# Attention output sums of a two-layer model: full-precision matmuls for the differential heads, one matmul per block with stationary values for the stick-breaking heads

## Chip, cores and metric

The kernel runs on one core of one Trainium2 chip. The metric is the device time of one execution in microseconds (us), the median of several runs; before the change it is 3962.36 us over three runs.

## What is computed

Two layers over 2048 tokens of width 1024. The first has three token mixers side by side (a pooling mixer, differential attention, stick-breaking attention) and a gated feed-forward network; the second has a gated spatial mixer and retention. The change touches the sums of values in the two attentions of the first layer:

```python
# differential attention, 4 heads; two softmaxes of width 64, values of width 128
attn = p[:, :, 0] - lam * p[:, :, 1]
outs.append(jnp.einsum('bhqk,bkhe->bqhe', attn, vb))
# stick-breaking attention, 4 heads of width 64, strictly causal
suffix = lax.cumsum(log_1mb, axis=3, reverse=True) - log_1mb
a = jnp.where(mask, jnp.exp(jax.nn.log_sigmoid(z) + suffix), 0.0)
outs.append(jnp.einsum('bhqk,bkhd->bqhd', a, vb))
```

Both are causal: a tile of 128 queries reads only the keys up to its own end.

## The kernel before

All data is float32. TensorE has a reduced format, fp32r, and the kernel keeps precision by splitting a number x into hi (x rounded to fp32r) and lo (x - hi, in fp32r) and adding up products: three matmuls for a projection (`product`, L1325 to L1327), fewer where one side needs less.

**Order of the work.** `order_of_work` runs once, in Python, and writes out a list of steps; each engine's program takes the steps of its own kinds in that order and waits for the others by semaphores. Two generators are interleaved: `projections` (all dense products, norms and gates) and `attention`. Their yields carry planned costs (`softmax_cost`, `sticks_cost`), by which attention steps are spread between the dense ones. `in_halves(n, fn)` puts a step n half-steps later. None of the costs is changed.

**Attention** goes through the 2048 tokens in four chunks c of 512 (CT). Heads j = 0 to 3 are the differential ones; j = 4 and 5 are pairs of stick-breaking heads, r = 0 and 1 in a pair. For each head and each tile qt of 128 queries it walks over blocks kb of keys of width w (512, or 128 to 512 on the diagonal). For a block:

- `scores` (L1424, L1425): TensorE, into PSUM bank 4 or 5;
- the weights: for differential heads a maximum on VectorE, Exp on ScalarE (L1649), a scaling on GpSimd and the difference of the two maps on VectorE (L1961); for stick-breaking heads logs, a scan and an Exp;
- `turn_p` (L1433): TensorE turns the weights in pieces of 128 columns, by transposes into PSUM bank 6. There is one such bank (`tring`, one place), so the next `turn_p` waits until bank 6 has been read;
- `split_p`: ScalarE copies bank 6 as hi (L1662), VectorE then writes lo = bank 6 - hi (L1967), both into tile PT, which has two places (`pt`);
- `pv` (L1447, L1449), two half-steps after `turn_p`: the turned weights are stationary, the values stream past them. For each 128 keys hi is loaded and streams [values hi, values lo], then lo is loaded and streams values hi. A differential head has 128 value columns, so 256 and 128 columns stream; a stick-breaking head has 64, so 128 and 64 stream. All add up in PSUM bank 7 (`oring`, one place);
- `take_out` (L1976), at the end of a tile: VectorE adds the halves of bank 7 into OB. The next tile's first `pv` waits for it.

There are 16 query tiles per head and 136 pieces of 128 by 128 (16 * 17 / 2), so 544 pieces for the four differential heads and 544 for the four stick-breaking ones. By blocks that is 160 each: 112 of four pieces, and 16 each of one, two and three.

When a head is done, `finish_head` squares it on ScalarE (L1690), norms and stores it.

**Values.** The value projection leaves a 128 by 512 bank; ScalarE writes hi to a staging tile, VectorE lo (`store_v`, L1884), and ScalarE's queue stores both to the DRAM scratch VS (`put_v`). `load_v` on the sync engine's queue (SP) loads 512 KB per block into the KV buffer.

The change's names in the order tables below: BIG, WF and W are operands of the dense products, KV and QQ keys, values and queries, PP the weights before they are turned, PT and PTW the turned ones, CB constants (the identity matrix among them), OB the head outputs, PS PSUM.

## Time and profile before

| | |
|---|---|
| three runs | 3962.36, 3954.04, 3963.06 us (median 3962.36) |
| span of the profiled execution | 3954.2 us |
| TensorE busy | 3727.1 us (94%), mean granted clock 0.978 |
| TensorE weight loads | 3270.0 us (83%) |
| VectorE, ScalarE, GpSimd busy | 1989.4, 1700.0, 799.3 us |
| HBM | 591.49 MB read, 179.59 MB written |

The profile comes from one execution. Its page gives the span, from the first to the last record, and no separate total for that execution; the median of the runs stands 8.2 us above the span. "PE" is TensorE's matmuls, "PEld" its weight loads, which overlap the matmuls. The duration of a matmul record contains its way through the pipeline, so matmuls that follow each other overlap in the records: what a matmul costs is read from the distance between starts. Line numbers (L1447) are those of the kernel before.

### The profile page before, as it was taken

The page shows a single profiled execution, that of the slowest core. Times are in us where ns is not written, and L with a number is a line of the kernel's source. Part 1 is how long each engine was busy: PE and PEld are TensorE (multiplying, and loading weights), DVE is VectorE, ACT ScalarE, POOL GpSimd, SP SyncE. Part 2 cuts the span into 40 slices and gives each one's busy share as a digit, 9 for nine tenths or more (in the row PEclk, how much of TensorE's full clock was granted, in tenths as well). Part 3 has the DMA queues.
Part 4 walks back from the last instruction along what each step waited for, and adds up shares of the span by engine and source line. Part 5 has one row for each costly group of instructions (what it writes and reads, how often), then busy time and mean ns, then how long its engine had stood idle before and what let it go on. Part 6 is the DMA issues. An engine that isn't in the chain of part 4 may idle for free.

```text
span 3954.2 us, 56218 instructions
## 1 busy us (share of the span) xinstructions
PE 3727.1 (94%) x21768; PEld 3270.0 (83%) x21768; DVE 1989.4 (50%) x4259; ACT 1700.0 (43%) x3455; POOL 799.3 (20%) x704
## 2 busy tenths in 40 slices
PE   7999899999998999999999999999999989999998
PEld 6888788787878887888888987888879987888897
DVE  4446575556646565555646545444566743101343
ACT  4334455556644444445544434334555543111322
POOL 3443333454444331100001000111000000000100
PEclk9999999999999999999999999999999999999999
DMA  6886667676666567454444555555353445555453
GB/s 171 276 270 184 191 206 276 223 266 233 241 238 210 208 208 277 173 174 165 164 171 159 176 192 208 181 181 179 132 201 124 142 157 212 192 192 191 163 187 143
DMA packets 327706, 774.76 MB, mean 196 GB/s; under 512 B 36241, under 2 KB 212369, under 8 KB 271122
## 3 DMA queue, kind: packets, MB, share of 16 engines
q1 hardware_dynamic: 266386, 731.31, 53.2%
q10 hardware_dynamic: 61056, 39.86, 3.6%
q8 instruction: 174, 2.85, 0.3%
q14 instruction: 90, 0.74, 0.1%
HBM read 591.49 MB, written 179.59 MB: 195 GB/s over the span
## 4 chain that ended last, share of the span: by engine, by line
PE 71%; DVE 12%; ACT 8%; issue 3%; DMA 2%; ACTq 2%; POOL 1%; SPq 0%; DVEq 0%
PE PS L1325 19%; PE PS L1327 19%; PE PS L1326 19%; PE PS L1447 3%; PE PS L1433 3%; PE PS L1425 2%; PE PS L1424 2%; PE PS L1449 2%; DVE PT L1967 1%; POOL WF L2225 1%; DVE SM L1935 1%; ACT WF L1547 1%; DVE BIG L1866 1%; ACT PT L1662 1%; ACT BIG L1604 1%
## 5 line engine op out<-in xcount | busy, mean ns | idle before, releaser
L1325 PE MATMUL PS<-WF,BIG 128*128 128x256 f32 (+1 forms) x2328 | 731.8, 314 | 21.1 <-POOL WF L2225 10.5
L1326 PE MATMUL PS<-WF,BIG 128*128 128x256 f32 (+1 forms) x2328 | 715.2, 307 | 0.0
L1327 PE MATMUL PS<-WF,BIG 128*128 128x256 f32 (+1 forms) x2328 | 714.9, 307 | 0.0
L1325 PE MATMUL PS<-BIG,WF 128*128 128x512 f32 (+1 forms) x1792 | 692.3, 386 | 20.4 <-DVE BIG L1866 9.5
L1327 PE MATMUL PS<-BIG,WF 128*128 128x512 f32 (+1 forms) x1792 | 677.7, 378 | 0.0
L1326 PE MATMUL PS<-BIG,WF 128*128 128x512 f32 (+1 forms) x1792 | 677.0, 378 | 0.0
L2225 POOL TENSOR_TENSOR WF<-RAW,WF 128x512 fp32r<-128x512 f32 x380 | 506.9, 1357 | 769.9 <-ACT WF L1547 769.7
L1967 DVE TENSOR_TENSOR PT<-PS,PT 128x512 fp32r<-128x512 f32 (+3 forms) x320 | 194.9, 609 | 616.3 <-ACT PT L1662 615.3
L1325 PEld LDWEIGHTS PS<-WF,BIG 128*128 128x128 f32 x2328 | 453.2, 195 | 48.6 <-POOL WF L2225 9.4
L1326 PEld LDWEIGHTS PS<-WF,BIG 128*128 128x128 f32 x2328 | 453.8, 195 | 22.4 <-issue 2.4
L1327 PEld LDWEIGHTS PS<-WF,BIG 128*128 128x128 f32 x2328 | 453.0, 195 | 18.9
L1649 ACT ACTIVATE PP<-PS,SM 128x512 f32<-128x512 f32 (+3 forms) x320 | 199.1, 622 | 566.8 <-DVE SM L1935 563.1
L1325 PEld LDWEIGHTS PS<-BIG,WF 128*128 128x128 f32 x1792 | 342.4, 191 | 82.2 <-ACT BIG L1604 7.7
L1327 PEld LDWEIGHTS PS<-BIG,WF 128*128 128x128 f32 x1792 | 341.9, 191 | 65.8
L1326 PEld LDWEIGHTS PS<-BIG,WF 128*128 128x128 f32 x1792 | 342.8, 191 | 59.6 <-issue 0.5
L2252 POOL TENSOR_TENSOR AT<-XS,AT 128x512 fp32r<-128x512 f32 x88 | 114.3, 1299 | 1103.9 <-ACT AT L1706 1103.9
L1447 PE MATMUL PS<-KV,PT 128*128 128x256 f32 (+1 forms) x1088 | 268.0, 311 | 57.7 <-DVE PT L1967 34.1
L1662 ACT ACTIVATE PT<-PS 128x512 fp32r<-128x512 f32 (+3 forms) x320 | 169.2, 529 | 344.0 <-PE PS L1433 333.1
L1447 PEld LDWEIGHTS PS<-KV,PT 128*128 128x128 f32 x1088 | 211.4, 194 | 77.7 <-DVE OB L1976 37.8
L1449 PE MATMUL PS<-KV,PT 128*128 128x128 f32 (+1 forms) x1088 | 250.5, 238 | 0.0
L1547 ACT ACTIVATE WF<-RAW 128x1024 fp32r<-128x1024 f32 x190 | 199.4, 1052 | 118.5 <-issue 80.7
L2010 DVE TENSOR_TENSOR XH<-PS,XH 128x512 f32<-128x512 f32 x224 | 150.6, 685 | 198.0 <-PE PS L1327 197.5
(220 smaller groups left out, 6809.1 us busy)
## 6 DMA issues: line engine op xcount, KB each, us to landing
WF<-scratch_WS SPq DMA_DIRECT2D x264, 1024.0 KB, 5.1
scratch_WS<-WF SPq DMA_DIRECT2D x110, 1024.0 KB, 6.6
W<-scratch_WS SPq DMA_DIRECT2D x66, 1024.0 KB, 5.0
RAW<-in_w_in SPq DMA_DIRECT2D x84, 512.0 KB, 4.5
KV<-scratch_KS SPq DMA_DIRECT2D x60, 512.0 KB, 6.0
KV<-scratch_VS SPq DMA_DIRECT2D x60, 512.0 KB, 4.7
QQ<-scratch_QS SPq DMA_DIRECT2D x192, 128.0 KB, 4.9
XH<-in_x SPq DMA_DIRECT2D x32, 512.0 KB, 6.3
```

Of the source, the lines that this page charges most:

```text
L1325: pe.matmul(o, Ah, Bh, start=first, stop=False)
L1326: pe.matmul(o, Ah, Bl, start=False, stop=False)
L1327: return pe.matmul(o, Al, Bh, start=False, stop=last)
L1433: m = pe.transpose(PS[6][:, 128 * i:128 * i + 128], src[:, 128 * i:128 * i + 128], ident)
L1447: pe.matmul(o, hi[:, 128 * i:128 * i + 128], vv[:, i, :, e0:e0 + en], start=first and i == 0 and r == 0, stop=False, skip_group_check=True)
L1449: m = pe.matmul(o[:, 0:en], lo[:, 128 * i:128 * i + 128], vv[:, i, 0, e0:e0 + en], start=False, stop=last and i == w // 128 - 1, skip_grou ...
L1547: act.activation(half_of(n)[0], rawp(n), ACT.Copy).then_inc(*inc("w_hi", ("w_hi", n)))
L1649: act.activation(probs(s)[:, 0:w], PS[4 + b][:, 0:w], ACT.Exp, bias=nm, accum_out=sm).then_inc(*inc("p_exp", ("ex", x, r)))
L1662: act.activation(turned(s)[0][:, 0:w], PS[6][:, 0:w], ACT.Copy).then_inc(*inc("p_hi", ("th", x, r)))
L1967: dve.tensor_tensor(lo, PS[6][:, 0:w], hi.bitcast(F32), ALU.subtract).then_inc(*inc("p_lo", ("tl", x, r)))
L2010: dve.tensor_tensor(dst, PS[b][:, :], dst, ALU.add).then_inc(*inc("residual", ("res", u)))
L2225: pool.tensor_tensor(lo, rawp(n)[:, 512 * i:512 * i + 512], hi.bitcast(F32), ALU.subtract).then_inc(*inc("w_lo", ("w_lo", n, i)))
```

## The change

- Differential heads: the turned weights are copied whole, as float32, into a tile PTW of four places (`keep_p`, ScalarE); VectorE's lo for them is gone. `pv` is one float32 matmul for each piece of 128 keys, weights stationary, 128 value columns streaming. Values are stored and loaded whole (VW, 256 KB a block). `take_out` becomes a plain copy.
- Stick-breaking heads: `pv_sb` is one fp32r matmul for each piece, with the values [hi, lo] of a head (64 + 64 columns) stationary and the turned weights [hi, lo] (128 + 128 columns) streaming, into a bank whose rows are value columns and whose columns are queries. At the end of a tile `fold_out` (VectorE) adds the two halves of columns into a place in PP, `turn_out` (TensorE) turns that back by two transposes into bank 6, and `take_turned` (VectorE) adds the hi and lo halves into OB. `turn_out` takes its place in the ring of bank 6, two half-steps (FB) after `fold_out`.
- Values of stick-breaking heads are stored head by head, in rows of 64 instead of 128 numbers.

```diff
-                            return ("ql", u)
+                            return ("ql" if idx == 2 else "qh", u)
                         s, before = staged.take(("qst", u))
                         do(("store_v", c, u, b, s, before, 2 * idx, g))
                         put_later(("put_v", c, u, s, 2 * idx, g))
...
         pch = Ring(10, [(("tables",),)] * 10)
-        pt = Ring(2)
+        pt = Ring(4)
         ob_after = [(), ()]
+        fold_after = [(), ()]
         heads = [(c, j) for c in range(NC) for j in range(6)]
         tiles = [(c, j, qt) for c, j in heads for qt in range(4)]
...
             o_before = ()
+            j, qt = x["j"], x["qt"]
             if x["first"] and r == 0:
-                _, o_before = oring.take(("o2", c, x["j"], x["qt"]))
-            do(("pv", c, x["x"], r, x["j"], x["qt"], x["kb"], x["w"], x["s"], vslot[c, x["j"], x["kb"]], en, x["first"],
-                x["last"], o_before))
+                _, o_before = oring.take(("o2" if en == 128 else "of", c, j, qt))
+            do(("pv" if en == 128 else "pv_sb", c, x["x"], r, j, qt, x["kb"], x["w"], x["s"], vslot[c, j, x["kb"]],
+                x["first"], x["last"], o_before))
             if r == 128 // en - 1:
                 if x["qt"] == 3:
                     released["v"].append(("pv", x["x"], r))
                     load_ahead()
                 if x["last"]:
-                    (take_out(c, x, r, en) if c == 0 else in_halves(1, lambda: take_out(c, x, r, en), True))
+                    take = take_out if en == 128 else fold_out
+                    (take(c, x, r, en) if c == 0 else in_halves(1, lambda: take(c, x, r, en), True))
 
         def take_out(c, x, r, en):
-            do(("take_out", c, x["x"], r, x["j"], x["qt"], en, ob_after[x["j"] % 2]))
+            do(("take_out", c, x["x"], r, x["j"], x["qt"], ob_after[x["j"] % 2]))
             if x["qt"] == 3:
                 in_halves(1, lambda: finish_head(c, x["j"]))
 
+        def fold_out(c, x, r, en):
+
+            j, qt = x["j"], x["qt"]
+            do(("fold_out", c, x["x"], r, j, qt, fold_after[qt % 2]))
+            fold_after[qt % 2] = (("ot", c, j, qt),)
+
+            def turn_back():
+                _, before = tring.take(("o2", c, j, qt))
+                do(("turn_out", c, j, qt, before))
+                do(("take_turned", c, j, qt, ob_after[j % 2]))
+                if qt == 3:
+                    in_halves(1, lambda: finish_head(c, j))
+            in_halves(FB, turn_back)
+
         def turn(x, r, src, made):
-            b, bbefore = tring.take(("tl", x["x"], r))
+            b, bbefore = tring.take(("tl", x["x"], r) if x["j"] > 3 else ("tw", x["x"]))
             x["s"], sbefore = pt.take(("pv", x["x"], r))
             do(("turn_p", x["x"], r, x["w"], src, made, bbefore))
-            do(("split_p", x["x"], r, x["w"], x["s"], sbefore))
+            do(("split_p" if x["j"] > 3 else "keep_p", x["x"], r, x["w"], x["s"], sbefore))
 
         yield "proj", 0
         load_ahead()
...
-            aslot, cslot = Ring(7, pch.held[:7]), Ring(3, pch.held[7:])
+            aslot, cslot = Ring(6, pch.held[:6]), Ring(3, pch.held[7:])
+            fold_after[0] = fold_after[1] = pch.held[6]
+            pt = Ring(2, [pt.held[2 * i] + pt.held[2 * i + 1] for i in range(2)])
...
+            pt = Ring(4, [pt.held[i // 2] for i in range(4)])
             att_done.add(c)
 
...
         PP = sbt("PP", 5120)
+        with ExitStack() as lay:
+            PTW = sbt("PTW", 2048, F32, lay)
...
             return PT[:, 1024 * s:1024 * s + 512], PT[:, 1024 * s + 512:1024 * s + 1024]
+
+        def whole(s):
+            return PTW[:, 512 * s:512 * s + 512]
+
+        def whole_values_of(kb):
+            return KVF[:, 2048 * kb + 1024:2048 * kb + 1536]
+
+        def turned_both(s):
+            return PT[:, 1024 * s:1024 * s + 1024].rearrange("p (a t) -> p a t", a=2)
+
+        def folded(qt):
+            return PP[:, 3072 + 256 * (qt % 2):3328 + 256 * (qt % 2)]
 
...
 
-            def pv(c, x, r, j, qt, kb, w, s, vs, en, first, last, o_before):
+            def pv(c, x, r, j, qt, kb, w, s, vs, first, last, o_before):
                 on.wait_ge("v", c, j, kb)
                 for e in o_before:
                     on.wait_ge(*e)
+                on.wait_ge("tw", x)
+                vv = whole_values_of(vs).rearrange("p (t e) -> p t e", t=4)
+                for i in range(w // 128):
+                    m = pe.matmul(PS[7][:, 0:128], whole(s)[:, 128 * i:128 * i + 128], vv[:, i, :], start=first and i == 0,
+                                  stop=last and i == w // 128 - 1, skip_group_check=True)
+                m.then_inc(*inc("weighed", ("pv", x, r)))
+
+            def pv_sb(c, x, r, j, qt, kb, w, s, vs, first, last, o_before):
+                on.wait_ge("v", c, j, kb)
+                for e in o_before:
+                    on.wait_ge(*e)
                 on.wait_ge("th", x, r)
                 on.wait_ge("tl", x, r)
-                vv = values_of(vs).rearrange("p (t a e) -> p t a e", t=4, a=2)
-                hi, lo = turned(s)
-                e0 = en * r
-                o = PS[7][:, 128 * r:128 * r + 2 * en]
+                vv = values_of(vs).rearrange("p (t r m) -> p t r m", t=4, r=2)
+                pp = turned_both(s)
+                o = PS[7][:, 256 * r:256 * r + 256].rearrange("p (a q) -> p a q", a=2)
                 for i in range(w // 128):
-                    pe.matmul(o, hi[:, 128 * i:128 * i + 128], vv[:, i, :, e0:e0 + en], start=first and i == 0 and r == 0,
-                              stop=False, skip_group_check=True)
-                    m = pe.matmul(o[:, 0:en], lo[:, 128 * i:128 * i + 128], vv[:, i, 0, e0:e0 + en], start=False,
-                                  stop=last and i == w // 128 - 1, skip_group_check=True)
+                    m = pe.matmul(o, vv[:, i, r, :], pp[:, :, 128 * i:128 * i + 128],
+                                  start=first and i == 0 and r == 0, stop=last and i == w // 128 - 1, skip_group_check=True)
                 m.then_inc(*inc("weighed", ("pv", x, r)))
+
+            def turn_out(c, j, qt, before):
+                on.wait_ge("of", c, j, qt)
+                for e in before:
+                    on.wait_ge(*e)
+                for r in range(2):
+                    m = pe.transpose(PS[6][:, 128 * r:128 * r + 128], folded(qt)[:, 128 * r:128 * r + 128], ident)
+                m.then_inc(*inc("o_turned", ("ot", c, j, qt)))
 
             def ada_cols(b, before):
                 for e in before:
...
+                act.activation(to, PS[b][:, :], ACT.Copy).then_inc(*inc("qkv_hi", ("qh", u)))
 
             def put_u(c, u, s, f):
...
                 on.wait_ge("qh", u)
+                if ft < 4:
+                    for f in range(2):
+                        view = stage(s)[0].rearrange("p (u n) -> p u n", u=2)[:, :, 128 * f:128 * f + 128]
+                        act.dma_start(VW[ft + f, c, :, 2 * g:2 * g + 2, :], view.bitcast(F32)).then_inc(*landed(f"s_st{s}", ("qst", u)))
+                    return
                 on.wait_ge("ql", u)
                 for a, src in enumerate(stage(s)):
                     for f in range(2):
                         view = src.rearrange("p (u n) -> p u n", u=2)[:, :, 128 * f:128 * f + 128]
-                        act.dma_start(VS[ft + f, c, :, 2 * g:2 * g + 2, a, :], view.bitcast(F32)).then_inc(*landed(f"s_st{s}", ("qst", u)))
+                        by_head = VS[f, c, :, :, :, :].rearrange("p t a e -> p (t a e)").rearrange("p (t r a e) -> p t r a e", t=4, r=2, a=2)
+                        for i in range(2):
+                            act.dma_start(by_head[:, 2 * g + i, :, a, :],
+                                          view[:, i, :].rearrange("p (r e) -> p r e", r=2).bitcast(F32)).then_inc(*landed(f"s_st{s}", ("qst", u)))
 
             def soft_exp(x, r, m, kb, w, b, s, before, m_after):
                 nm, sm, _ = norm_cols(m, 4 * r + kb, 1)
...
+                on.wait_ge("tp", x, r)
+                for e in sbefore:
+                    on.wait_ge(*e)
+                act.activation(whole(s)[:, 0:w], PS[6][:, 0:w], ACT.Copy).then_inc(*inc("p_hi", ("tw", x)))
 
             def sb_logs(x, r, w, b, a_, before):
                 a = probs(a_)[:, 0:w]
...
             def store_v(c, u, b, s, sbefore, ft, g):
+                if ft < 4:
+                    return
...
 
-            def take_out(c, x, r, j, qt, en, O_before):
-                parts = 128 // en
-                dst = outs_of(j)[:, 128 * qt:128 * qt + 128].rearrange("p (r e) -> p r e", r=parts)
-                src = PS[7][:, 0:256].rearrange("p (r a e) -> p r a e", r=parts, a=2)
+            def take_out(c, x, r, j, qt, O_before):
                 on.wait_ge("pv", x, r)
+                for e in O_before:
+                    on.wait_ge(*e)
+                dve.tensor_copy(outs_of(j)[:, 128 * qt:128 * qt + 128],
+                                PS[7][:, 0:128]).then_inc(*inc("o_step", ("o2", c, j, qt)))
+
+            def fold_out(c, x, r, j, qt, before):
+                dst = folded(qt).rearrange("p (r q) -> p r q", r=2)
+                src = PS[7][:, :].rearrange("p (r a q) -> p r a q", r=2, a=2)
+                on.wait_ge("pv", x, r)
+                for e in before:
+                    on.wait_ge(*e)
+                dve.tensor_reduce(dst, src.rearrange("p r a q -> p r q a"), AX, ALU.add).then_inc(*inc("o_step", ("of", c, j, qt)))
+
+            def take_turned(c, j, qt, O_before):
+                dst = outs_of(j)[:, 128 * qt:128 * qt + 128].rearrange("p (r e) -> p r e", r=2)
+                src = PS[6][:, 0:256].rearrange("p (r a e) -> p r a e", r=2, a=2)
+                on.wait_ge("ot", c, j, qt)
                 for e in O_before:
                     on.wait_ge(*e)
                 dve.tensor_reduce(dst, src.rearrange("p r a e -> p r e a"), AX, ALU.add).then_inc(*inc("o_step", ("o2", c, j, qt)))
...
                     on.wait_ge(*e)
-                sp.dma_start(values_of(s).bitcast(F32), VS[j, kb, :, :, :, :].rearrange("p t a e -> p (t a e)")).then_inc(
-                    *landed(f"s_v{s}", ("v", c, j, kb)))
+                if j < 4:
+                    sp.dma_start(whole_values_of(s), VW[j, kb, :, :, :].rearrange("p t e -> p (t e)")).then_inc(*landed(f"s_v{s}", ("v", c, j, kb)))
+                else:
+                    sp.dma_start(values_of(s).bitcast(F32), VS[j - 4, kb, :, :, :, :].rearrange("p t a e -> p (t a e)")).then_inc(
...
     scr = {}
-    for name, shape in (("QS", [6, 16, 64, 2, 2, 128]), ("KS", [6, NC, 128, 2, CT]), ("VS", [6, NC, 128, 4, 2, 128]),
+    for name, shape in (("QS", [6, 16, 64, 2, 2, 128]), ("KS", [6, NC, 128, 2, CT]), ("VS", [2, NC, 128, 4, 2, 128]), ("VW", [4, NC, 128, 4, 128]),
```

How instructions move. TensorE, a differential block of two pieces in chunk 0, before:

```order
L1327 MATMUL PS<-BIG,WF 128x512
L1447 MATMUL PS<-KV,PT 128x256
L1449 MATMUL PS<-KV,PT 128x128
L1447 MATMUL PS<-KV,PT 128x256
L1449 MATMUL PS<-KV,PT 128x128
L1433 MATMUL PS<-CB,PP 128x128 x3
L1424 MATMUL PS<-KV,QQ 128x256
```

and with the change:

```order
L1364 MATMUL PS<-BIG,WF 128x512
L1480 MATMUL PS<-KVF,PTW 128x128 x2
L1470 MATMUL PS<-CB,PP 128x128 x3
L1461 MATMUL PS<-KV,QQ 128x256
L1462 MATMUL PS<-KV,QQ 128x256
```

Four matmuls become two; what stands around them is the same.

TensorE, a stick-breaking block of two pieces in chunk 0, just after a tile has ended, before:

```order
L1327 MATMUL PS<-BIG,WF 128x512
L1447 MATMUL PS<-KV,PT 128x128
L1449 MATMUL PS<-KV,PT 128x64
L1447 MATMUL PS<-KV,PT 128x128
L1449 MATMUL PS<-KV,PT 128x64
L1433 MATMUL PS<-CB,PP 128x128 x2
L1325 MATMUL PS<-BIG,WF 128x512
```

and with the change:

```order
L1364 MATMUL PS<-BIG,WF 128x512
L1494 MATMUL PS<-PT,KV 128x256 x2
L1470 MATMUL PS<-CB,PP 128x128 x2
L1503 MATMUL PS<-CB,PP 128x128 x2
L1362 MATMUL PS<-BIG,WF 128x512
```

The two transposes of `turn_out` (L1503) stand directly behind the transposes of the next block's `turn_p` (L1470), which use the same PSUM bank. In this form, with no matmul between, `turn_out` stands 7 times in chunk 0 and once in chunk 2; of the other 24, most have 9 to 12 dense matmuls in between.

VectorE at the same place, before:

```order
L1889 MEMSET XH 128x256
L1976 TENSOR_REDUCE OB<-PS 128x128
L1967 TENSOR_TENSOR PT<-PS,PT 128x256
L1982 SCALAR_TENSOR_TENSOR PP<-PS,PP 128x384
...
L1878 SCALAR_TENSOR_TENSOR STG<-PS,STG 128x512
L1967 TENSOR_TENSOR PT<-PS,PT 128x256
L1982 SCALAR_TENSOR_TENSOR PP<-PS,PP 128x384
```

and with the change:

```order
L1959 MEMSET XH 128x256
L2052 TENSOR_REDUCE PP<-PS 128x256
L2037 TENSOR_TENSOR PT<-PS,PT 128x256
L2066 SCALAR_TENSOR_TENSOR PP<-PS,PP 128x384
...
L1946 SCALAR_TENSOR_TENSOR STG<-PS,STG 128x512
L2037 TENSOR_TENSOR PT<-PS,PT 128x256
L2060 TENSOR_REDUCE OB<-PS 128x128
L2066 SCALAR_TENSOR_TENSOR PP<-PS,PP 128x384
```

`take_out` (L1976) has become `fold_out` (L2052) at its place and `take_turned` (L2060) behind the second `split_p` after it.

## Rows read from the trace of the kernel before

**Rows 1.** The page: busy time of each engine.

```profile
PE 3727.1 (94%) x21768; PEld 3270.0 (83%) x21768; DVE 1989.4 (50%) x4259; ACT 1700.0 (43%) x3455; POOL 799.3 (20%) x704
```

**Rows 2.** Windows: us, busy PE, PEld, DVE, ACT, POOL, clock, DMA share, GB/s.

```profile
480.00:600.00 120.00, 114.75 (x692) 101.11 (x691) 84.38 (x162) 66.53 (x157) 42.99 (x33) 0.99 0.66 203
```

**Rows 3.** Timeline of PE, a differential block of four pieces (start, length).

```profile
2130.05 0.28 PE L1447 MATMUL PS<-KV,PT 128*128 128x256 f32 x1
2130.23 0.33 PE L1447 MATMUL PS<-KV,PT 128*128 128x256 f32 x1
...
2130.91 0.62 PE L1433 MATMUL PS<-CB,PP 128*128 128x128 f32 x4
```

**Rows 4.** Timeline of PE, a stick-breaking block of four pieces.

```profile
2830.49 0.22 PE L1447 MATMUL PS<-KV,PT 128*128 128x128 f32 x1
2830.55 0.24 PE L1449 MATMUL PS<-KV,PT 128*128 128x64 f32 x1
2830.63 0.30 PE L1447 MATMUL PS<-KV,PT 128*128 128x128 f32 x1
...
2831.30 0.66 PE L1433 MATMUL PS<-CB,PP 128*128 128x128 f32 x4
2831.71 0.48 PE L1325 MATMUL PS<-BIG,WF 128*128 128x512 f32 x1
```

**Rows 5.** Timeline of PE, dense fp32r matmuls of 256 and of 512 columns.

```profile
1264.46 0.28 PE L1325 MATMUL PS<-WF,BIG 128*128 128x256 f32 x1
1264.58 0.28 PE L1326 MATMUL PS<-WF,BIG 128*128 128x256 f32 x1
...
1500.18 0.39 PE L1327 MATMUL PS<-WF,BIG 128*128 128x512 f32 x1
1500.40 0.39 PE L1325 MATMUL PS<-WF,BIG 128*128 128x512 f32 x1
```

**Rows 6.** Timeline of PEld, float32 matmuls of the retention branch (L1503, L1507).

```profile
1256.72 0.98 PEld L1503 LDWEIGHTS PS<-GB 128*128 128x128 f32 x8
1257.61 0.97 PEld L1507 LDWEIGHTS PS<-XS 128*128 128x128 f32 x8
```

**Rows 7.** Groups by line and shape, PE: count, busy us, mean ns.

```profile
L1503 PE MATMUL PS<-GB 128*128 128x128 f32 x128 | 18.4, 289 | 5.2 <-ACT XS L1725 3.4 <-ACT GB L1746 1.8
L1433 PE MATMUL PS<-CB,PP 128*128 128x128 f32 x1088 | 188.0, 289 | 2.8 <-DVE PP L1961 2.8
```

**Rows 8.** Timeline, chunk 0: the turning of a block, and its subtract on VectorE.

```profile
533.09 0.66 PE L1433 MATMUL PS<-CB,PP 128*128 128x128 f32 x4
534.22 3.26 DVE L1902 TENSOR_TENSOR XH<-XH 128x527 f32<-128x527 f32 x3
540.17 0.68 DVE L1967 TENSOR_TENSOR PT<-PS,PT 128x512 fp32r<-128x512 f32 x1
```

**Rows 9.** The same where nothing else is queued, at the end of attention.

```profile
3217.37 0.60 ACT L1662 ACTIVATE PT<-PS 128x512 fp32r<-128x512 f32 x1 [3.08 <-PE PS L1433]
3218.00 0.69 DVE L1967 TENSOR_TENSOR PT<-PS,PT 128x512 fp32r<-128x512 f32 x1 [0.86 <-ACT PT L1662]
3218.83 0.44 PE L1447 MATMUL PS<-KV,PT 128*128 128x128 f32 x1 [1.50 <-DVE PT L1967]
```

**Rows 10.** Timeline of PE, and a window behind it, columns as in rows 2.

```profile
3214.64 0.32 PE L1447 MATMUL PS<-KV,PT 128*128 128x128 f32 x1 [4.00 <-DVE PT L1967]
...
3215.00:3220.00 5.00, 3.50 (x17) 3.12 (x16) 2.76 (x4) 1.11 (x2) 0.00 (x0) 0.50 0.00 0
```

**Rows 11.** Who waited for whom on PE: us in total, times, longest.

```profile
PE PS L1447 <- DVE PT L1967: 34.1, 20, 4.4
PE PS L1447 <- DVE OB L1976: 20.3, 10, 3.9
```

**Rows 12.** Groups by shape on VectorE, columns as in rows 7.

```profile
L1967 DVE TENSOR_TENSOR PT<-PS,PT 128x512 fp32r<-128x512 f32 x224 | 154.5, 690 | 480.4 <-ACT PT L1662 479.9
L1976 DVE TENSOR_REDUCE OB<-PS 128x128 f32<-128x256 f32 x96 | 39.8, 414 | 14.5 <-PE PS L1449 14.4
```

15 lines of the change are left out of this document (9 added, 6 removed).

## The prediction

> **What bounds the kernel now.** I read the busy times first. TensorE is busy for 3727 of 3954 us, every other engine for half of the span or less [rows 1]; in the window where chunk 0's stick-breaking heads run it is still busy for 115 of 120 us [rows 2]. So a nanosecond taken from TensorE's stream counts nearly whole, and VectorE's or ScalarE's time counts only where TensorE waits for it.
>
> Next I read what the matmuls of this change cost, from the distance of their starts. A differential block of four pieces starts at 2130.05 and the transposes behind it at 2130.91: 0.86 us. Its first piece takes 0.18, each later one 0.23 (its first weight load lies under the matmul ahead) [rows 3]. A stick-breaking block takes 0.81 us, 0.14 for the first piece and 0.223 for each later one [rows 4]. That the second streams half as many columns and costs the same says that weight loads bind here, two to a piece, some 0.115 us each. A dense fp32r matmul with its load costs 0.12 us for 256 columns and 0.22 for 512 [rows 5].
>
> **Float32 matmuls** are the crux, and the trace has some of just the new shape: 128 stationary, 128 streaming, in `ret_scores` (L1503). Eight records start within 0.89 us, 0.111 each [rows 6]. But `ret_scores` issues 4 such matmuls for each of 4 heads in 4 chunks, 64, and the trace has 128 records; transposes, also float32, have 1088 records for the 1088 pieces [rows 7]. So a plain float32 matmul is two records, 0.222 us, and a transpose is one. Whoever takes the mean of a record for that of an instruction finds the change twice as good as it is for the differential heads.
>
> Last, the waits of `pv`: 34 us for VectorE's lo and 20 us for `take_out`, of both kinds of heads together [rows 11].
>
> **The change, part by part.**
>
> *Stick-breaking sums* (gain). One load and 256 streaming fp32r columns a piece: 0.12 us [rows 5]. A block of four goes from 0.81 to 0.48, 0.33 saved, times 112 blocks = 37.0 us. Blocks of one, two and three pieces (16 each) cost 0.14, 0.36 and 0.59 now (0.14 + 0.223 for each further piece, [rows 4]) and 0.12, 0.24, 0.36 then: 0.37 * 16 = 5.9 us. Together **-43**.
>
> *Differential sums* (about nothing). A block of four goes from 0.86 to 8 * 0.111 = 0.89: 0.03 * 112 = 3.4 us more. Shorter blocks cost 0.174, 0.404, 0.634 before (0.174 is the first piece with its last step) and 0.222, 0.444, 0.666 then: 0.12 * 16 = 1.9. Together **+5**. The bounds are one record, 0.111 a piece, which is nearly 60 less, and two records that do not overlap a neighbour, 10 ns more each, which is +11 more; I take the middle, since the count of records decides.
>
> *Turning back.* 64 transposes; four cost 0.41 us with what follows [rows 4], so some 0.11 each: **+7**.
>
> *Waits of `turn_out`.* It needs bank 6 after `split_p` of the block just turned, ScalarE's copy and VectorE's subtract. With nothing queued, copy, subtract and the handing over keep TensorE idle for 1.5 us [rows 9]. In chunk 0 `turn_out` stands 7 times directly behind those transposes, and there both engines have other work queued ahead: in rows 8 the transposes start at 533.09 and the subtract ends at 540.85, because pooling (L1902) stands ahead of it on VectorE. Before, nobody needed it until 541.0. I laid the seven places on the trace: from where `turn_out` would stand to the end of the subtract there are 2.9, 2.1, 7.5, 7.0, 3.8, 2.0 and 1.7 us, 27 us (0.1 of hand-over each included). The fourth has a head's squares ahead on ScalarE, and these come later with the change, and each wait lets the two engines catch up: I take 20. The other 25 places have 9 or more dense matmuls in between, 1.1 to 2.7 us by rows 5, mostly enough for copy and subtract; where they are not, the same reading finds 6 us, of which I take 4. Queued behind the waiting transposes are dense matmuls, and `take_turned` on VectorE. Bounds: 7 times the unloaded 1.5 us, 10, and all of 33. Together **+24**, with their bounds 10 to 33.
>
> *Clock.* After TensorE had stood for 4 us, the next window shows the granted clock at 0.50, that is 1.2 instead of 2.4 GHz [rows 10]. Long waits bring that, so the three or four longest ones may cost a us or two each: **+3** (0 to 8).
>
> *VectorE's part of `pv`'s wait.* Differential heads lose the subtract, 0.69 us at full width [rows 12], so where TensorE waits for it, up to 0.8 us go. I count eleven such places in the differential heads; in four of them, the two longest among them, `take_out` ended only 0.3 to 0.5 us earlier, so no more than that is won there. **-7** (0 to -15).
>
> *VectorE's relief.* 160 subtracts (112 * 0.69 + 16 * 1.26 = 97 us) and 16 of the value projection at 0.69 go. `fold_out` reduces 512 columns where `take_out` reduced 256 in 0.414 [rows 12]; the price is between that and twice that, so up to 13 us more over 32 tiles. VectorE is half idle, so this counts only where TensorE waits behind its queue: **-5** (0 to -15).
>
> *At nothing:* ScalarE's copies (as many, as wide); its queue's stores (96 before and after); half the bytes of 40 value loads, since each load is issued ahead of its block and no `pv` waits for one in rows 11; `fold_out` at the end of a tile, because bank 7 is asked for again two half-steps later (at worst 0.3 us on each of the few tiles where VectorE is late now).
>
> Sum: -43 + 5 + 7 + 24 + 3 - 7 - 5 = **-16**. The profiled execution has 3954.2 us of span; its own total is not shown. The median of the runs is 8.2 above the span, and I keep that: 3962.4 - 16 = **3946 us**.
>
> *A rule that speaks against the change.* The starts in rows 3 and 4 show that loads bind, whatever streams. The Trainium skill (TensorE: Matmul & The Clock Gate, Back-to-back issue gap) gives N / 2.4 + 2.5 ns for a matmul by itself, by streaming columns alone, and by that stick-breaking sums would cost more than before, since 192 columns become 256 for each piece: a rival below. For a stream of loads and matmuls the same section gives about 81 ns at N = 128; by that a stick-breaking piece would cost 162 before at most, and the trace, with 223, does not agree. The page's load of P / 1.2 = 107 ns (its section LDWEIGHTS) lies near the measured 0.115.
>
> **Rivals.**
>
> 1. *`turn_out` hardly waits* because the engines catch up: 8 instead of 24 us, and no clock cost: -43 + 5 + 7 + 8 - 7 - 5 = -35, 3927. For it: where TensorE is held, its helpers lose their backlog. Against: the pooling ahead of the subtract does not go away [rows 8].
> 2. *The waits eat the gain*: all 33 us, clock 8, no relief: -43 + 5 + 7 + 33 + 8 - 7 = +3, so 3965, no change.
> 3. *Slower: bank 6 becomes the bound in every tile.* `turn_out` waits for the split, and the next `turn_p` for `take_turned`, and the block's whole chain (scores, scan, weights) behind it shifts. At the unloaded 1.5 us for the first and about 0.5 for the second, 32 tiles cost 64 us on top of the backlog of chunk 0 (another 10): -43 + 5 + 7 + 74 - 12 = +31, 3993. It decides from about 43 us of waits on, 1.3 us a tile. Against it: outside chunk 0 nearly all tiles have dense work between.
> 4. *Streaming columns bind, not loads* (the rule above). By rows 5 a column costs 0.10 / 256 = 0.4 ns and a matmul some 15 ns besides. Then a stick-breaking piece now has the floor 192 * 0.4 + 30 = 107 ns and 120 with the change, +7 us in all, and differential ones 184 to 222, +20. With the other terms: +27 + 7 + 24 + 3 - 12 = +49, 4011. Rows 3 and 4 speak against it: measured starts, not floors, are what goes away.
> 5. *A float32 matmul costs one record*: 55 more saved, 3886. Rows 7 speak against it.
>
> **How the numbers follow.** A measurement of this kernel can tell about 0.3%, 12 us, from no change, so faster means below 3950. My forecast, 3946 give or take 12, has 0.52, of which 0.36 lies below 3950 and 0.16 within 0.3%. Rival 1 has 0.22 (faster), rival 2 0.12 (same), rival 3 0.09 and rival 4 0.02 (slower), rival 5 0.03 (faster). That makes 0.61 faster, 0.28 same, 0.11 slower. For 8 in 10 the range takes the forecast, rivals 1 and 2 and their bounds: 3915 to 3974.
>
> **What would show it.** Right: `pv` of differential heads has 1088 records (two for each of 544), a four-piece block from its first start to the transposes takes 0.87 to 0.92 us; `pv_sb` has 544 records, 0.12 apart; TensorE waits for some 15 to 30 us before L1503, in chunk 0 mostly, for VectorE's L2037; the window of chunk 0's stick-breaking heads is longer than before, that of chunk 3's shorter by 18 us (43 * 58 / 136, its share of the pieces). Wrong: 544 records for L1480; waits before L1503 in every tile; new waits before L1494 for the fold; a granted clock well below 0.978.

## The result, and the profile after

| | before | after |
|---|---|---|
| median of the runs | 3960.32 us (6 runs, 3951.03 to 3969.91) | 3976.49 us (6 runs, 3970.81 to 3982.29) |
| ratio, 95% interval | | 1.0044 (1.0028 to 1.006) |
| span of the profiled execution | 3954.2 us | 3972.5 us |

Slower by 0.44%, just beyond the 0.3% that the prediction takes for no change, and well within 2%. The page's busy times of the changed kernel:

```profile
span 3972.5 us, 55010 instructions
PE 3702.7 (93%) x21288; PEld 3239.2 (82%) x21288; DVE 1903.5 (48%) x4115; ACT 1701.9 (43%) x3455; POOL 794.0 (20%) x704
```

And the core's row with the granted clock:

```profile
core 0: 3972.5 us, clock 0.970
```

TensorE has less to do and yet ends later [rows 1]. Three numbers split a span: what TensorE stood idle (span less busy), what the half clock cost ((1 - granted clock) times span), and the rest, its work at full clock. Before: 3954.2 - 3727.1 = 227 idle, 0.022 * 3954 = 87 clock, rest 3640. After: 270 idle, 0.030 * 3972.5 = 119 clock, rest 3583. So the work became **57 us shorter, the idle time 43 us longer, and the clock took 32 us more**: +18. The clock's term and the rest are good to some 2 us, since the clock is given to three digits.

The clock's term is an upper bound, because it also charges the half clock to time in which TensorE stood idle. Counted in the clock records of the two traces only where TensorE was busy, the half clock costs 73 us before and 95 after, 22 more, and the work falls from 3655 to 3608, by 46. The 43 us of idle time are the same in both counts.

The matmuls themselves, as groups by line (shapes, count, busy us, mean ns, idle before them):

```profile
L1480 PE MATMUL PS<-KVF,PTW 128*128 128x128 f32 x1088 | 150.2, 278 | 12.7 <-ACT PTW L1730 9.5 <-DVE OB L2043 3.2
L1494 PE MATMUL PS<-PT,KV 128*128 128x256 f32 x544 | 98.7, 298 | 54.3 <-DVE PP L2052 34.8 <-DVE PT L2037 16.1 <-issue 3.1
```

A differential and a stick-breaking block in TensorE's timeline (start, us, instruction):

```profile
671.17 1.05 PE L1480 MATMUL PS<-KVF,PTW 128*128 128x128 f32 x8
672.06 0.38 PE L1470 MATMUL PS<-CB,PP 128*128 128x128 f32 x2
...
2836.06 0.64 PE L1494 MATMUL PS<-PT,KV 128*128 128x256 f32 x4
2836.54 0.60 PE L1470 MATMUL PS<-CB,PP 128*128 128x128 f32 x4
2836.89 0.42 PE L1461 MATMUL PS<-KV,QQ 128*128 128x384 f32 x1
```

1088 records for 544 float32 matmuls, and a four-piece block from its start to the next instruction takes 0.89 us; the stick-breaking block takes 0.48 where it took 0.81 [rows 3, 4]. The four transposes behind it take 0.35 instead of 0.41.

Whom TensorE waited for (us in total, times, longest):

```profile
PE PS L1494 <- DVE PP L2052: 34.8, 13, 4.8
PE PS L1440 <- DVE BIG L1934: 25.7, 18, 5.2
PE PS L1503 <- DVE PT L2037: 23.5, 8, 7.5
PE PS L1494 <- DVE PT L2037: 16.1, 10, 4.0
PE PS L1470 <- DVE PP L2031: 10.4, 5, 4.1
PE PS L1480 <- ACT PTW L1730: 9.5, 7, 4.4
PE PS L1480 <- DVE OB L2043: 3.2, 2, 1.7
```

The wait for `split_p` before `turn_out` (L1503) is the one forecast. The largest is another: `pv_sb` (L1494) waits 34.8 us for `fold_out` (L2052), which I had put at nothing. Before, `take_out` held TensorE for 20.3 us over both kinds of heads [rows 11]. And `turn_p` (L1470) waits 10.4 us for the differential weights (L2031), which the change does not touch.

Lining both traces up by their 16128 dense matmul records shows where (times are those of the changed kernel). Up to record 2000 (448 us) it is 11 us ahead; at 2400 (573 us) it is 10 us behind, so chunk 0's stick-breaking heads cost 21; at 7600 and 11200 (2943 us) it is back within 3 us; at 12800 (3305 us), behind chunk 3's stick-breaking heads, 19 behind, and so to the end. The first is `turn_out` in chunk 0. In windows (length, busy and instructions of PE, PEld, DVE, ACT, POOL, clock, DMA):

```profile
480.00:600.00 120.00, 95.26 (x536) 82.99 (x534) 76.89 (x131) 53.99 (x116) 34.12 (x27) 0.93 0.55 160
3000.00:3120.00 120.00, 113.79 (x904) 111.00 (x902) 81.21 (x193) 62.15 (x107) 3.13 (x2) 0.98 0.45 156
```

and the second window in the kernel before:

```profile
3000.00:3120.00 120.00, 120.00 (x994) 118.05 (x993) 84.26 (x200) 64.98 (x112) 4.69 (x3) 1.00 0.45 151
```

Where [rows 2] had 114.75 of 120 us busy there are 95.26 now, and the clock is 0.93. Chunk 3's stick-breaking heads, to which the second window belongs, I had expected to be 18 us *shorter* than before; TensorE was busy there throughout, and now stands idle for 6 of 120 us. VectorE's timeline there (start, us, instruction):

```profile
3046.33 0.41 DVE L2224 TENSOR_TENSOR GB<-XS,GB 128x256 f32<-128x256 f32 x1
...
3050.14 0.42 DVE L2233 TENSOR_TENSOR XS<-XS,GB 128x256 f32<-128x256 f32 x1
3050.47 0.68 DVE L2052 TENSOR_REDUCE PP<-PS 128x256 f32<-128x512 f32 x1
```

and TensorE's (idle before it in brackets):

```profile
3040.45 0.64 PE L1494 MATMUL PS<-PT,KV 128*128 128x256 f32 x4
3051.21 0.51 PE L1494 MATMUL PS<-PT,KV 128*128 128x256 f32 x2 [3.69 <-DVE PP L2052]
```

The tile's sums end at about 3041; `fold_out` begins at 3050.47, behind twelve operations of the rotary step (L2224 to L2233), 4.1 us of them. In the kernel before, the reduce of that place stood ahead of the rotary step, as VectorE's timeline shows:

```profile
3034.33 0.41 DVE L1976 TENSOR_REDUCE OB<-PS 128x128 f32<-128x256 f32 x1
...
3043.13 0.41 DVE L2140 TENSOR_TENSOR GB<-XS,GB 128x256 f32<-128x256 f32 x1
```

The next `pv` there started at 3037.25, so the reduce had 2.5 us to spare, and the rotary step came 8 us behind it. So not the price of an instruction changed here but **what stands ahead of it**. Comparing the two written-out lists of steps from end to end shows why. `finish_head` of a stick-breaking head is now called from `turn_back`, two half-steps later. `attention` empties a chunk's leftovers with `while any(soon): yield from half(0.8)`, and it now needs two half-steps more: 12, 13, 13, 13 instead of 10, 11, 11, 11 in the four chunks. Each one is planned at a cost of 0.8, by which the dense work advances against the attention. From chunk 1 on nearly every attention step meets other dense steps: 270 of the 288 `pv` steps of chunks 1 to 3 have another number of dense product steps ahead of them than before, and none of chunk 0's 32. At the first `pv` of the last tile of head 2 in chunk 3 there are 1171 instead of 1164, at that of the last stick-breaking tile 1485 instead of 1481.

### The profile page after: what moved, and what is told of

Its sections match the earlier page's. It is cut to its first block, busy times and chain, and to the rows that moved or that the text cites. A ratio compares the mean times of both kernels' runs of the same rounds, so it can differ in the third digit from the quotient of the medians.

```text
span 3972.5 us, 55010 instructions
## 1 busy us (share of the span) xinstructions
PE 3702.7 (93%) x21288; PEld 3239.2 (82%) x21288; DVE 1903.5 (48%) x4115; ACT 1701.9 (43%) x3455; POOL 794.0 (20%) x704
## 4 chain that ended last, share of the span: by engine, by line
PE 52%; DVE 7%; ACT 4%; issue 2%; POOL 0%; DMA 0%; SPq 0%; ACTq 0%; DVEq 0%
PE PS L1362 14%; PE PS L1364 14%; PE PS L1363 14%; PE PS L1470 2%; PE PS L1480 2%; PE PS L1462 1%; PE PS L1461 1%; PE PS L1494 1%; DVE PP L2080 1%; DVE PT L2037 0%; PE PS L1440 0%; DVE GB L1922 0%; ACT GB L1608 0%; DVE GB L2286 0%; ACT BIG L1657 0%
## 5 line engine op out<-in xcount | busy, mean ns | idle before, releaser
L2005 DVE TENSOR_REDUCE SM<-PS 128x1 f32<-128x512 f32 (+3 forms) x320 | 194.4, 608 | 247.6 <-PE PS L1462 243.0
L1362 PE MATMUL PS<-WF,AT 128*128 128x512 f32 x584 | 240.6, 412 | 9.9 <-DVE XH L2094 7.0
L1363 PE MATMUL PS<-WF,AT 128*128 128x512 f32 x584 | 235.1, 403 | 0.0
L2037 DVE TENSOR_TENSOR PT<-PS,PT 128x512 fp32r<-128x512 f32 (+3 forms) x160 | 97.6, 610 | 286.6 <-ACT PT L1724 286.4
L1364 PE MATMUL PS<-WF,AT 128*128 128x512 f32 x584 | 234.5, 402 | 0.0
```

The costliest lines, as they stand in the source:

```text
L1362: pe.matmul(o, Ah, Bh, start=first, stop=False)
L1363: pe.matmul(o, Ah, Bl, start=False, stop=False)
L1364: return pe.matmul(o, Al, Bh, start=False, stop=last)
L2005: dve.tensor_reduce(nm, PS[4 + b][:, 0:w], AX, ALU.max, negate=True).then_inc(*inc("row_max", ("mx", x, r)))
L2037: dve.tensor_tensor(lo, PS[6][:, 0:w], hi.bitcast(F32), ALU.subtract).then_inc(*inc("p_lo", ("tl", x, r)))
```

## The experiments

Each number is the median, with the ratio to the kernel before in the same comparison (3960.87, 3958.95 and 3957.32 us in the three). In the first two, theory A puts the loss on the waits of `turn_out` and of the fold, wherever the steps stand, and theory B on the moved order; from e3_diff_only on each text names its own theories. None leaves a part of the computation out.

**e1_order.** The kernel before, with the order of all other steps as the change makes it:

```diff
-                in_halves(1, lambda: finish_head(c, x["j"]))
+                in_halves(1 if x["j"] < 4 else 3, lambda: finish_head(c, x["j"]))
```

> The kernel before, with one edit: stick-breaking heads are finished two half-steps later, which makes the order of all other steps the same as in the changed kernel (the change had moved it without meaning to). Theory A (the waits of turn_out and of the fold are the loss, wherever the steps stand): 3960 give or take 4, like before. Theory B (the moved order alone puts take_out behind long VectorE work in chunk 3 and costs the loss): 3972 to 3985, with 12 us or more of waits for L1976 after 2800 us.

4029.7 us, 1.018 (1.0162 to 1.0198). Not one matmul is changed, and 69 us are lost. Theory A is refuted, and theory B had the direction but not the size, 45 us more than its upper bound. The list of steps, without those that the change adds or replaces and without the finishing of heads, is step by step that of the changed kernel. Its waits, against [rows 11]:

```profile
PE PS L1447 <- DVE OB L1976: 41.9, 21, 4.2
PE PS L1447 <- DVE PT L1967: 33.3, 18, 4.4
PE PS L1433 <- DVE PP L1961: 14.2, 5, 4.1
```

The wait for `take_out` doubled, the one for the lo did not grow.

**e2_old_order.** The whole change, its extra half-steps planned at no cost, so that the old interleaving stays:

```diff
+            n = 0
             while any(soon):
-                yield from half(0.8)
+                n += 1
+                yield from half(0.8 if n <= (11 if c else 10) else 0.0)
```

> The changed kernel, with the two added half-steps at the end of each chunk's attention planned at no cost, so that dense products and attention interleave as before the change. Theory A: 3976 give or take 5, with the waits for the fold (L2052) still 30 us or more. Theory B: 3950 to 3962, the waits for the fold back to some 10 us, the waits before turn_out in chunk 0 (24 us) unchanged.

3946.98 us, 0.9964 (0.995 to 0.9978): 29 us below the change as made, a little faster than before, and 3 us below theory B's range.

```profile
PE PS L1505 <- DVE PT L2039: 35.7, 11, 7.5
PE PS L1496 <- DVE PP L2054: 18.7, 8, 4.7
PE PS L1472 <- DVE OB L2062: 13.5, 9, 4.2
```

(Lines are two further here: L1505 is `turn_out`, L1496 `pv_sb`, L1472 `turn_p`.) The fold's wait is nearly halved, but is not back to the 10 us of theory B. `turn_out` waits as long as before in chunk 0 (22.9 us at seven places) and 12.9 us more at four places of later chunks, and `turn_p` waits for `take_turned` (L2062) to free bank 6.

**e3_diff_only.** Only the differential half of the change; the stick-breaking `pv` and `take_out` are those of before, and so is the order:

```diff
-    take = take_out if en == 128 else fold_out
+    take = take_out
...
-    m = pe.matmul(o, vv[:, i, r, :], pp[:, :, 128 * i:128 * i + 128], ...)
+    pe.matmul(o, hi[:, 128 * i:128 * i + 128], vv[:, i, :, e0:e0 + en], ...)
+    m = pe.matmul(o[:, 0:en], lo[:, 128 * i:128 * i + 128], vv[:, i, 0, e0:e0 + en], ...)
```

> The differential heads' part alone (float32 matmuls, whole values, plain take_out), stick-breaking heads as before, order of the work as before. By the forecast's terms: +5 for two records a piece, -7 and -5 for VectorE's lo gone, so 3953 give or take 6. If two records a piece cost more beside other work than in ret_scores: 3965 or more. If waits count nearly twice, because the clock falls after them: 3945.

3906.6 us, 0.9868 (0.9852 to 0.9885): 54 us faster, though its matmuls are no shorter, and 38 us below the lowest of the three values expected. The waits before `pv` (L1495 sticks, L1479 differential):

```profile
PE PS L1495 <- DVE PT L2037: 13.0, 8, 4.0
PE PS L1495 <- DVE OB L2050: 10.0, 5, 3.6
PE PS L1479 <- DVE OB L2044: 8.9, 4, 2.9
PE PS L1479 <- ACT PTW L1730: 5.0, 7, 0.9
```

Together 37 of the 54 us of before [rows 11].

**e4_sticks_only.** Only the stick-breaking half, in the moved order that it brings; the differential `pv` has hi and lo as before.

```diff
-    m = pe.matmul(PS[7][:, 0:128], whole(s)[:, 128 * i:128 * i + 128], vv[:, i, :], ...)
+    pe.matmul(o, hi[:, 128 * i:128 * i + 128], vv[:, i, :, e0:e0 + en], ...)
+    m = pe.matmul(o[:, 0:en], lo[:, 128 * i:128 * i + 128], vv[:, i, 0, e0:e0 + en], ...)
```

> The stick-breaking heads' part alone (one matmul a piece, fold, turn_out), differential heads as before, in the moved order. Forecast's terms: -43 + 7 + 27 = -9, 3951. Theory A with the clock's share (waits for turn_out and fold 50 us, half clock 25 to 30 us more): 3980 to 3990, that is the whole loss and what the differential part wins.

4046.89 us, 1.0224 (1.0207 to 1.0241). That is 57 us above what was expected, which had no cost of the moved order in it. Against e1_order, which has the same order, it is 17 us slower with 49 us less work. Its waits for the fold and before `turn_out`:

```profile
PE PS L1499 <- DVE PP L2057: 35.0, 13, 4.8
PE PS L1508 <- DVE PT L2040: 26.1, 8, 7.5
```

**e5_turn_early.** e2_old_order with `turn_out` a half-step nearer to the fold in chunk 0:

```diff
-            in_halves(FB, turn_back)
+            in_halves(FB if c else FB - 1, turn_back)
```

> Kernel e2 (the changed kernel in the old order), with turn_out one half-step after the fold in chunk 0 instead of two, so that one or two groups of dense matmuls stand between it and the transposes of the block's turn_p; other chunks unchanged. e2 measured 3947. Theory A (the waits before turn_out in chunk 0, some 27 us, and the clock's fall behind them, some 10 more): 3905 to 3918. Rival (ScalarE and VectorE are behind in chunk 0 anyway, and the wait only moves to the next pv): 3935 or more.

3931.89 us, 0.9933 (0.9921 to 0.9946), 15 us below e2_old_order, and between the two forecasts:

```profile
PE PS L1472 <- DVE OB L2062: 24.0, 14, 7.4
PE PS L1505 <- DVE PT L2039: 17.4, 9, 4.8
```

The wait before `turn_out` fell by 18 us; that of `turn_p` for `take_turned` rose by 10. The two together went from 49 to 41: bank 6 is held by one or the other.

**e6_fold_early.** e5_turn_early with the fold directly behind the tile's last `pv_sb` in all chunks, `turn_back` still the same distance from the tile's end for chunks 1 to 3:

```diff
-    (take(c, x, r, en) if c == 0 else in_halves(1, ..., True))
+    (take(c, x, r, en) if c == 0 or en == 64 else in_halves(1, ..., True))
...
-            in_halves(FB if c else FB - 1, turn_back)
+            in_halves(FB + 1 if c else FB - 1, turn_back)
```

> e5, and in chunks 1 to 3 the fold is issued right behind the tile's last pv_sb instead of a half-step later, so that it stands earlier in VectorE's queue (turn_out stays where it was). If the waits for the fold (19 us in e2, 8 places) come from other work ahead of it on VectorE: 12 to 25 us below e5. If VectorE then stands waiting for the pv in front of other work: e5 or slower.

3913.62 us, 0.9887 (0.9871 to 0.9902): 18 us less than e5, inside the 12 to 25 expected. The wait of `pv_sb` for the fold, 18.7 us in e5, is gone; those of bank 6 went from 24.0 and 17.4 to 27.1 and 20.8 us.

**e7_dummy_reduce.** e3_diff_only with an idle reduce of as many columns on VectorE in each place where a subtract went:

```diff
+            def keep_p(x, r, w, s, sbefore):
+                on.wait_ge("tw", x)
...
+                dve.tensor_reduce(SM[:, 204:205], CB[:, 0:w], AX, ALU.max).then_inc(*inc("p_lo", ("dum", x)))
```

> e3 (differential part alone, 3907), with a reduce over 128 to 512 columns of constants put on VectorE in the place of each of the 160 subtracts that the change took away; nobody waits for its result. If e3 gains because VectorE is lighter and all that stands behind in its queue is earlier: 3925 to 3945. If it gains because pv no longer waits for VectorE's part: within 6 us of e3.

3942.56 us, 0.996 (0.9948 to 0.9973): 36 of e3's 54 us are given back. TensorE waits for none of these reduces; they only push back what stands behind them in VectorE's queue. They do so in two ways that this run does not separate: by their own time, and because each first waits for ScalarE's copy, as the subtract did, and holds up the queue behind it. The group of the full-width ones, with 76.7 us of work and 268.9 us of VectorE's idle time before them:

```profile
L2041 DVE TENSOR_REDUCE SM<-CB 128x1 f32<-128x512 f32 x112 | 76.7, 685 | 268.9 <-ACT PTW L1730 268.8
```

and the wait that grew most of those before `pv`, from 8.9:

```profile
PE PS L1479 <- DVE OB L2053: 16.1, 8, 4.1
```

The other 18 us of e3 belong to what else the differential half changes: `pv` no longer waits for the lo, PTW has four places instead of two, the value loads are half as long and the value projection has 16 subtracts less. These were not taken apart.

**e8_diff_take_early.** e3_diff_only with bank 7's reader directly behind the last `pv` of every tile, and `finish_head` kept where it was:

```diff
-    (take(c, x, r, en) if c == 0 else in_halves(1, lambda: take(c, x, r, en), True))
+    take(c, x, r, en)
...
-    in_halves(1, lambda: finish_head(c, x["j"]))
+    in_halves(2 if c else 1, lambda: finish_head(c, x["j"]))
```

> e3 with take_out right behind the tile's last pv in all chunks (both kinds of heads), finishing a head where it was. e3 still waits 19 us for take_out (9 places). If other work ahead of it on VectorE is the cause: 3890 to 3900. If VectorE then waits in front of other work: 3907 or more.

**3881.11 us, 0.9806 (0.9791 to 0.9821): the fastest of all, about 2% faster than both kernels,** and 9 us below the range expected. Its stick-breaking `pv` no longer waits for `take_out`; 13.6 us for the lo remain, and 7.6 us in which the differential `pv` waits for the copy out of bank 7.

The last four cross these factors; their edits are those shown above, in other company.

**e9_late_finish_free_drain.** e1_order with the drain of e2_old_order.

> The kernel before with finish_head of the stick-breaking heads two half-steps later, as in e1_order, but the drain half-steps beyond before's number are planned at no cost, so that the attention and the dense work keep their old interleaving. Theory (the 69 us of e1_order come from the longer drain, which moves all work after chunk 0 against each other): within 6 us of before, 3953 to 3965, clock 0.977 to 0.979. Rival (the heads' finishing, squares and scaling, two half-steps later, is what collides): 4000 or more, waits as in e1_order.

3959.93 us, 1.001 (1.0 to 1.002). `finish_head` is as late as in e1_order, and that costs 3 us (0 to 8 by the interval). So nearly all of the 69 us come from the drain's planned cost.

**e10_diff_moved_order.** e3_diff_only with the one line of e1_order.

> e3_diff_only (whole values and whole probabilities in the differential heads alone) in the moved order of e1_order. Theory A (the order decides which works meet in VectorE's queue, and the lost subtracts make that queue shorter in either order): the moved order costs less here than the 69 us it costs the kernel before, 20 to 50, so 3927 to 3957. Rival B (two separate effects that add): 3906.6 + 69 = 3976, near the changed kernel's own 3976 although no stick-breaking sum is changed. Rival C (only the subtracts that are late matter, none is left): 3915 or less.

3963.39 us, 1.0019 (1.001 to 1.0028): the moved order costs 57 us here, between A (20 to 50) and B (69). A shorter queue on VectorE protects little, 12 of 69 us.

```profile
PE PS L1495 <- DVE OB L2050: 26.6, 13, 4.2
PE PS L1469 <- DVE PP L2031: 11.5, 4, 4.1
```

These rows are 10.0 and 2.0 us in e3_diff_only. The changed kernel shows the same two, 34.8 us for bank 7's reader (13 times there too) and 10.4 for the weights.

**e11_before_take_early.** The kernel before with the two lines of e8_diff_take_early.

> The kernel before with take_out directly behind the tile's last pv in every chunk and not one half-step later, all else in the old order. Theory A (bank 7's reader stands late in VectorE's queue; what e8 won over e3, 25 us, was this): 3925 to 3945, waits before the first pv of a tile for take_out (20 us in before) under 8. Rival B (with the subtracts still in the queue the earlier reduce pushes them back, and the wait for lo grows as much): 3955 to 3970.

3935.41 us, 0.9947 (0.9934 to 0.9959): 22 us from moving one step. Its wait for `take_out`, 20.3 us before, is gone; that for the lo rose only from 34.1 to 37.6.

**e12_take_early_both.** e6_fold_early with the same two lines, so that the differential copy is early too.

> e6_fold_early with the differential heads' copy also directly behind the last pv: both parts of the change, the old order, all readers of bank 7 early. Theory A (the effects add, the sticks' matmuls are worth 55 us and their waits cost most of it): 3913.6 - 25 = 3889, 3882 to 3896, not below e8_diff_take_early. Rival B (with the waits for bank 7 gone the stick-breaking part keeps over 20 us of its 55): 3865 or less, the best of all. Rival C (other waits take their place): 3905 or more.

3909.98 us, 0.9883 (0.987 to 0.9897). Rival C's time: no better than e6 (0.9887) that can be told from noise, and 29 us worse than e8. Theory A's 25 us counted a part twice: of e8's gain over e3 the larger wait, 10.0 us, was that of the stick-breaking `pv`, and e6 already has the fold early. What was left to win was the differential `pv`'s wait for the copy, 6.1 us in e6. The two waits at bank 6 are those of e6 (27.1 and 20.8 us):

```profile
PE PS L1472 <- DVE OB L2062: 27.4, 15, 7.4
PE PS L1505 <- DVE PT L2039: 19.6, 10, 4.7
```

47 us at bank 6, which e8 has not. So these are not new waits in the place of others, as rival C had it, but the ones that the earlier readers never touched.

**All runs, split as above** (us; the median is over the runs, the rest is of the profiled execution; idle = span - TensorE busy, clock = (1 - granted clock) * span, work = the rest):

| | median | idle | clock | work |
|---|---|---|---|---|
| before | 3960 | 227 | 87 | 3640 |
| e9 late finish, free drain | 3960 | 229 | 91 | 3638 |
| e11 take early | 3935 | 212 | 87 | 3636 |
| e1 moved order | 4030 | 271 | 121 | 3634 |
| e3 differential | 3907 | 190 | 74 | 3642 |
| e7 the same, dummy reduces | 3943 | 215 | 91 | 3638 |
| e8 e3, take early | 3881 | 179 | 66 | 3639 |
| e10 e3, moved order | 3963 | 228 | 95 | 3638 |
| e4 sticks, moved order | 4047 | 320 | 137 | 3585 |
| **after** (both, moved order) | 3976 | 270 | 119 | 3583 |
| e2 both, old order | 3947 | 255 | 107 | 3584 |
| e5 e2, turn early | 3932 | 248 | 98 | 3586 |
| e6 e5, fold early | 3914 | 235 | 86 | 3590 |
| e12 e6, copy early | 3910 | 234 | 90 | 3584 |

The work has two levels, about 3638 with the old stick-breaking sums and 3585 with the new, whatever the order. Everything else is idle time and clock. With the half clock counted only where TensorE was busy, the levels are 3652 to 3655 and 3607 to 3611, and the clock costs from 53 us (e8) to 112 (e4).

## Why the prediction was wrong

The forecast was 3946, the time 3976, 2 us above the range and on the side that had 0.11. In the old order the same change takes 3947 (e2_old_order). That agreement is partly luck, as the terms show.

1. **"What stands around them is the same" and "None of the costs is changed"**, ahead of the prediction, and `finish_head` nowhere in the sum, though the prediction notes that the squares of a head come later with the change. This step failed, and it decided the sign. I compared a few stretches of the order in chunk 0 and at a tile, where it is the same, and not its whole length. The moved order costs 29 us in the changed kernel (3976.5 against 3947.0), 57 with the differential part alone (e10 against e3), and 69 in the kernel before (e1), where e9 pins it on the drain's planned half-steps. No rival had it. Why it costs only 29 us in the changed kernel is not shown.

2. **`fold_out` "at nothing"**, because bank 7 is asked for two half-steps later, "at worst 0.3 us on each of the few tiles where VectorE is late now". Priced by its own duration, it is cheap: 0.68 us. What counts is what stands ahead of it on VectorE, 4.1 us in the place shown. Late readers of bank 7 cost 34.8 us before L1494; putting the reader first was worth 22 us in the kernel before (e11), 25 with the differential part (e8 against e3) and 18 in e6; the differential copy alone, in e12, brought nothing clear of noise.

3. **VectorE's part of `pv`'s wait, -7, and relief, -5**: mis-sized. With the matmuls' +5 they make -7 for the differential part; it gives -54 (e3_diff_only), of which e7_dummy_reduce puts 36 on VectorE's queue alone: on the time of what no longer stands in it, and on its waiting there for ScalarE's copy. "VectorE is half idle, so this counts only where TensorE waits behind its queue" was right as a sentence; but the waits for VectorE in other places than `pv` were not counted.

4. **Clock, +3 (0 to 8)**: measured +32, or +22 if only the half clock of TensorE's busy time counts; both lie outside. I gave it to the three or four longest waits. In these runs it goes with the idle time as a whole: +43 idle and +32 clock after, +44 and +34 in e1, +93 and +50 in e4, -37 and -13 in e3, -48 and -21 in e8. It is not strictly so (e11: -15 and 0), but a microsecond more of idle time came with up to 0.8 us more of clock (up to 0.6 by the narrower count). No run changes the clock by itself, so this is how the two go together, not a price.

5. **The matmuls, -43 + 5 + 7 = -31**: the mechanism right, the gain larger, 57 by the table and 46 by the narrower count of the clock. Alone, the differential part adds 2 to the work (e3 against before; 0 by the narrower count) and the stick-breaking part takes 49 (e4 against e1) to 58 from it (e2 against e3; 44 to 47 by the narrower count). 0.48 us for a four-piece block and 0.89 for a differential one are as forecast; the transposes behind a stick-breaking block take 0.06 us less each time (112 full blocks, 7 us), which no term had, and turning back costs 0.14 us a tile, 4 us in place of 7. With these two the sum is -41; what is left to 46 stays open. Rivals 4 and 5 fell with it. For rival 4's rule (the Trainium skill, TensorE: Matmul & The Clock Gate, Back-to-back issue gap) the new pieces, 256 columns and 0.118 apart, lie near its 109 ns; the old ones stood at 0.223 a pair where it gives 85 ns, so in this trace it tells the cost only where columns are many for each load.

6. **`turn_out`'s waits, +24 (10 to 33)**: 23.5 us, 8 times, the longest 7.5, seven of them in chunk 0 as said. The seven places, forecast at 2.9, 2.1, 7.5, 7.0, 3.8, 2.0 and 1.7 us, took 2.5, 2.8, 7.5, 3.9, 3.6, 1.2 and 1.4. In the old order there are 35.7, four places of later chunks more. The places were laid on the trace one by one, and in chunk 0 that held.

7. **Rival 3**, bank 6 as the bound, has a true half. The wait of `turn_p` for `take_turned` is 13.5 us in e2 and 27.4 in e12, with `turn_out`'s own 19.6. That is 47 us, over the 43 that I gave as its point of decision, though at some places and not in every tile. With the stick-breaking part the kernel is 10 to 13 us slower in the moved order (after against e10, by the ratios or the medians), 40 in the old (e2 against e3), and 29 with early readers (e12 against e8), in spite of 45 to 58 us less work in each. In the last pair the idle time differs by 55 us, and 47 of these stand at bank 6; that it is bank 6 which keeps the part from paying is read from these waits, and no run took them away.

Two of the prediction's own signs of being wrong appeared: new waits before L1494 for the fold (34.8 us) and a granted clock well below 0.978 (0.970). Its signs for the matmuls, 1088 and 544 records, 0.89 us a block and 0.12 us a piece, came as said.

So the two parts of the change pull apart: the differential part, whose matmuls gain nothing, wins 54 us, 36 of them by what it takes from VectorE's queue; the stick-breaking part, whose matmuls gain some 45 to 55, loses 10 to 40 by what it adds to bank 6 and VectorE, and 29 more go to the order that it moves. The stick-breaking part alone in the old order was not run, and whether a second bank in bank 6's place would let it pay was not tried.

## What to carry to other kernels

Where a program writes out its own order, compare the whole of it, on every engine, before pricing anything: a callback that comes two half-steps later moved all that followed, and cost more (29 us) than the edit itself won in the old order (14 us). Price a reader of a shared PSUM bank by what stands ahead of it in its engine's queue, not by its own duration, and put it directly behind the last matmul; that alone was worth 18 to 25 us in three kernels here, and nothing in a fourth where its wait was already small. Split each span into idle, clock and work before explaining it: it shows in three numbers whether an edit shortened the work or only changed the waits.

## What the runs showed of the hardware

- The granted clock falls with short waits as well: in chunk 0's stick-breaking heads, where the longest wait is 7.5 us and most are under 4, the mean clock went from 0.99 to 0.93. Behind a single wait of 2.52 us, matmuls of 512 columns start 0.43 us apart for some 3 us, and then 0.23 again (rows below). Kernels whose idle time stood some 40 us or more above or below that of before had a third to 0.8 of that in clock as well (0.3 to 0.6 if only busy time counts); small differences didn't follow it (the table).
- Four transposes of float32 behind an fp32r block of four single matmuls take 0.35 us to the next instruction; behind hi and lo pairs they took 0.41 [rows 4]. Why was not tried.
- Reduces that nobody's sums need, 0.69 us at full width, 160 of them (76.7 us in the 112 full ones), each behind a wait for ScalarE's copy, on an engine that is busy for half of the span, cost 36 us of the kernel's time.

The clock behind a short wait, in the changed kernel's TensorE timeline:

```profile
2854.43 0.79 PE L1494 MATMUL PS<-PT,KV 128*128 128x256 f32 x3 [2.52 <-DVE PP L2052]
...
2856.08 0.63 PE L1363 MATMUL PS<-WF,AT 128*128 128x512 f32 x1
2856.51 0.63 PE L1364 MATMUL PS<-WF,AT 128*128 128x512 f32 x1
...
2858.18 0.39 PE L1362 MATMUL PS<-WF,AT 128*128 128x512 f32 x1
2858.41 0.39 PE L1363 MATMUL PS<-WF,AT 128*128 128x512 f32 x1
```
